# Last unit of a hybrid conv encoder step: W_in read as f32 and split on chip, another order of the gate pairs, later statistics of the first output tiles

## The chip, the cores and the metric

One core of one Trainium2 chip (trn2). The metric is the device time of one execution in microseconds (us). Three runs of the kernel before gave 1589.52, 1590.16 and 1591.43 us; their median is 1590.16 us. Engines: PE = TensorE (PEld its weight loads), DVE = VectorE, ACT = ScalarE, POOL = GpSimd, SP = SyncE, which here issues every DMA.

## What is computed

```python
hn = rms_norm(x, norm_g)                               # (4096 prompt + 32 sample rows, 1024)
proj = einsum('btd,de->bte', hn, w_in)                 # 1024 -> 3584, all f32
h_a, b_a, c_a, z_a, a_b, g_b, z_b = split(proj, 7)     # 512 wide each
conv_a = causal_dwconv(hist_a, c_a * h_a, conv_a_w)    # 3 taps
out_a = b_a * conv_a * silu(z_a)
v_b = a_b * sigmoid(g_b)
conv_b = causal_dwconv(hist_b, v_b, conv_b_w)          # 31 taps
s_b = silu(layer_norm(conv_b + bias, ln_b_g, ln_b_b))
out_b = s_b * silu(z_b)
y = x + concat([out_a, out_b]) @ w_out                 # then a final rms_norm
```

All inputs and outputs are f32. The new convolution histories are outputs too.

## The kernel before, in words

**Products.** Every f32 operand is split in a high part (a copy to fp32r, on ACT) and a low part (operand minus high part, on DVE or POOL); one product is three matmuls, high x high, high x low, low x high (`split_product`, L1733, its matmuls L1737 to L1739).

**Input projection.** 4140 columns of x (padding, sample, prompt) are 9 blocks of 460 columns. The 28 tiles of 128 output columns of `w_in` go in 14 pairs, in the order ORDER (L36): `ga` = g and a of group B, `hc` = h and c, `bz` = b and z, `zz` = two tiles of z_b, each with a number j from 0 to 3 (`zz`: 0 and 1). Unit 0 (periods 0 to 13) multiplies blocks 0 and 1 and also makes the forms of the weights: their split parts and the split sums of a seven-product scheme, eight chunks of 512 columns by two parts for each pair, which SP stores to DRAM as `weight_forms` (`store_forms`, L640) as two DMAs. Units 1 to 3 take two blocks each, with seven products for each pair (`strassen_product`, L1782). Unit 4, the last (periods III = 56 to 69, here called periods 0 to 13 of the last unit), takes block 8 alone: two tiles for each pair, each of two halves of 12 matmuls (`late_tile`, L1818), so 56 halves, numbered r. Each half reads one slot of the nine-slot ring `w_ring`; a slot holds 512 columns as high and low part, loaded from `weight_forms` (512 KB) by `load_late` (L663). Slots are reused nine halves later up to half 27, then only four slots turn (`late_slot`, L328), as the rest of that memory is taken for the output stage.

**What else goes on in the last unit.** ACT applies the function of the first tile of a pair (`evacuate`, L1160). DVE then multiplies the second tile in (`finish`, L1453): for `ga` one instruction (L1479), for `hc` one and three for the short convolution (L1503, L1506), for `bz` two (L1531, L1537). `zz` is ACT's alone. SP spills results to DRAM (`spill`, L670). The rest of DVE's time goes to the 31-tap convolution, one instruction per tap (L1554, the first L1551), each channel tile of a unit being a job of 31; `tap_quota` (L144) allows 12 per period, the first four before `finish`, and a job can begin one period after its `ga` pair. In ORDER the last unit's jobs 16 to 19 begin in its periods 1, 4, 8 and 11 and end in 3, 6, 10 and 13. POOL copies the history in front of each tile (`edges`, L945) and a `finish` waits for it. The first tap job of a pair waits for the same copy.

**Output stage.** Nine tiles of 512 rows (the last one is the sample). For each, layer norm over channels is 18 chained DVE steps and some on POOL, ACT and PE: `sums` and `sum_low` on POOL (L1006, L1017), `mean` on PE (L1847), `centre` on DVE (L1567), `squares` on ACT, `square_sums` and `var_low` on DVE (L1573, L1579), `var` on PE (L1851), `normalise` on DVE (L1585, L1590 to L1598), `silus` on ACT (L1224, L1228), `gate` (L1600), `mixed_b_high` on ACT (L1231), `b_low` (L1607). `a_low` (L1023, L1027) on POOL makes group A's low parts. For the first output tile all of this is placed in the last unit by hand: POOL's `sums` and `sum_low` in its period 3, PE's `mean` at the start of period 5 and `var` at the start of period 8, DVE's steps in the periods of `first_ln` (L1613). `W_out` is loaded, split and kept on chip (`out_weight_high`, `out_weight_low`) in periods 1 to 8.

Then nine steps (`run_steps`, L532) multiply row tiles of 128 rows (`rows_out`, L1878, 48 matmuls of 512 columns each), four to a step. PE's step L is: `mean(L+1)`, row tile 0, `var(L+1)`, row tiles 1, 2, 3. A row tile waits until DVE has added the residual of the tile two before (`need(pe, h_done, R - 1)`), and all row tiles of a step wait for its `b_low`. DVE's step L (L1693) is: `centre`, the finish of the last row tile, `square_sums`, `var_low`, `add_residual` of row tile 0, `normalise`, finish of 0, `add_residual` of 1, `gate`, finish of 1, `add_residual` of 2, `b_low`, finish of 2, `add_residual` of 3, where the layer norm is that of output tile L+1.

## Time and profile before

| | |
|---|---|
| median of three runs | 1590.16 us |
| the profiled execution: its time | 1589.94 us |
| its span in the trace | 1588.1 us |
| mean granted TensorE clock | 0.995 |
| PE busy | 1544.5 us, 97% |
| DVE busy | 1281.0 us, 81% |
| ACT, POOL busy | 509.0 us, 501.1 us, 32% each |
| DMA | 380 MB, mean 239 GB/s |

Times inside the trace count from the span's start. The profiled execution took 1.8 us more than its span. In the trace the last unit begins at about 1055.4 us and PE's last matmul of it starts at 1208.68 us; the output stage goes on to the end of the span. A line that shows "[idle <-releaser]" says how long the engine stood still before that instruction and what released it.

### The profile page before, as it was taken

Reading aid. Unit: us, or ns where it says so; the run is one execution under the profiler, and the core shown is the slowest. Engines: PE = TensorE matmul, PEld = TensorE weight load, DVE = VectorE, ACT = ScalarE, POOL = GpSimd, SP = SyncE. Lnnn points to the kernel's source line nnn. Section 1 sums busy time; section 2 is a strip of 40 time slices with the busy share of each in tenths; the row PEclk is TensorE's granted clock in tenths of the full one; section 3 lists DMA queues with packets and bytes.
Section 4 is the critical chain, followed back from the end, with each engine's and each line's share of the span. In section 5 each row is a group of like instructions: output and inputs, shape, how many; then the busy total and the mean of one; then the engine's idle time right before and its main releaser. Section 6 shows DMA issues by size and latency. Waiting matters only on the chain.

```text
span 1588.1 us, 19038 instructions
## 1 busy us (share of the span) xinstructions
PE 1544.5 (97%) x7196; PEld 1356.8 (85%) x7196; DVE 1281.0 (81%) x1196; ACT 509.0 (32%) x721; POOL 501.1 (32%) x434
## 2 busy tenths in 40 slices
PE   4899999999999999999999999999999999999998
PEld 4789999988888888888888888888887888888886
DVE  5699899997877998879798878785997777777752
ACT  4443433333333243332253312232231232323221
POOL 3756869201232221132221131113220333332310
PEclk9999999999999999999999999999999999999999
DMA  4898889689987788897779877779576443545441
GB/s 157 321 332 311 324 305 353 241 296 304 283 285 241 232 254 295 277 290 252 234 222 310 259 231 243 220 256 318 192 241 198 138 145 142 184 160 182 142 142 63
DMA packets 105613, 380.06 MB, mean 239 GB/s; under 512 B 16228, under 2 KB 20196, under 8 KB 101944
## 3 DMA queue, kind: packets, MB, share of 16 engines
q1 hardware_dynamic: 105528, 378.93, 71.4%
q8 instruction: 54, 0.88, 0.2%
q14 instruction: 31, 0.25, 0.0%
HBM read 277.70 MB, written 101.18 MB: 239 GB/s over the span
## 4 chain that ended last, share of the span: by engine, by line
PE 90%; DVE 6%; issue 2%; DMA 1%; POOL 1%; ACT 0%; POOLq 0%; DVEq 0%; SPq 0%; ACTq 0%
PE ps L1737 30%; PE ps L1739 30%; PE ps L1738 30%; DVE ps L1554 3%; DVE xf L1396 1%; DVE xf L1388 1%; DVE x_raw L1382 1%; DMA conv_b<-conv_spill 1%; DMA w_ring<-weight_forms 0%; PE ps L1844 0%; DVE w_ring L1396 0%; PE ps L1845 0%; POOL ln_tmp_a_f L1012 0%; POOL w_out_split L1032 0%; DVE conv_b L1571 0%
## 5 line engine op out<-in xcount | busy, mean ns | idle before, releaser
L1554 DVE SCALAR_TENSOR_TENSOR ps<-v,conv_b_taps,ps 128x920 f32<-128x920 f32 (+2 forms) x580 | 630.9, 1088 | 18.0
L1737 PE MATMUL ps<-xf,w_ring 128*128 128x460 f32 x1624 | 605.2, 373 | 3.3 <-DMA w_ring<-weight_forms 2.1
L1739 PE MATMUL ps<-xf,w_ring 128*128 128x460 f32 x1624 | 604.1, 372 | 0.0
L1738 PE MATMUL ps<-xf,w_ring 128*128 128x460 f32 x1624 | 602.7, 371 | 0.0
L1737 PEld LDWEIGHTS ps<-xf,w_ring 128*128 128x128 f32 x1624 | 306.4, 189 | 39.0 <-issue 3.3
L1738 PEld LDWEIGHTS ps<-xf,w_ring 128*128 128x128 f32 x1624 | 306.4, 189 | 34.7
L1739 PEld LDWEIGHTS ps<-xf,w_ring 128*128 128x128 f32 x1624 | 305.9, 188 | 35.1
L1172 ACT ACTIVATE sets<-ps 128x460 f32<-128x460 f32 x168 | 92.8, 552 | 460.3 <-PE ps L1739 456.5
L1737 PE MATMUL ps<-w_out_split,mixed 128*128 128x512 f32 x528 | 206.5, 391 | 0.0
L1739 PE MATMUL ps<-w_out_split,mixed 128*128 128x512 f32 x528 | 206.4, 391 | 0.0
L1738 PE MATMUL ps<-w_out_split,mixed 128*128 128x512 f32 x528 | 206.3, 391 | 0.0
L1002 POOL TENSOR_TENSOR sets<-sets 128x460 f32<-128x460 f32 x42 | 55.0, 1310 | 425.1 <-ACT sets L1172 425.1
L1737 PEld LDWEIGHTS ps<-w_out_split,mixed 128*128 128x128 f32 x528 | 99.5, 189 | 21.8 <-issue 1.0
L1739 PEld LDWEIGHTS ps<-w_out_split,mixed 128*128 128x128 f32 x528 | 99.5, 188 | 20.9
L1738 PEld LDWEIGHTS ps<-w_out_split,mixed 128*128 128x128 f32 x528 | 99.4, 188 | 20.8
L1342 ACT ACTIVATE ps<-h_rows 128x1024 f32<-128x1024 f32 (+1 forms) x33 | 34.0, 1029 | 213.6 <-DVE h_rows L1685 213.6
L879 POOL TENSOR_TENSOR row_mean_sq_eps<-row_mean_sq,rms_eps 128x1 f32<-128x1 f32 (+1 forms) x33 | 9.0, 274 | 282.2 <-ACT ps L1342 282.2
L1737 PE MATMUL ps<-xf 128*128 128x460 f32 x224 | 84.7, 378 | 10.8 <-DVE xf L1388 10.8
L1739 PE MATMUL ps<-xf 128*128 128x460 f32 x224 | 84.3, 376 | 0.0
L1738 PE MATMUL ps<-xf 128*128 128x460 f32 x224 | 83.6, 373 | 0.0
L905 POOL TENSOR_TENSOR x_raw<-x_raw,rstd_spread 128x460 f32<-128x460 f32 x56 | 69.4, 1272 | 44.9 <-DMA rstd_spread<-rstd_spill 44.9
L1685 DVE TENSOR_TENSOR h_rows<-ps,x_rows_again 128x1024 f32<-128x1024 f32 (+1 forms) x33 | 40.2, 1218 | 39.3 <-PE ps L1739 39.3
(144 smaller groups left out, 1575.0 us busy)
## 6 DMA issues: line engine op xcount, KB each, us to landing
w_ring<-weight_forms SPq DMA_DIRECT2D x350, 512.0 KB, 5.1
weight_forms<-xf SPq DMA_DIRECT2D x14, 2048.0 KB, 11.2
weight_forms<-w_ring SPq DMA_DIRECT2D x14, 2048.0 KB, 13.5
x_raw<-in_xT SPq DMA_DIRECT2D x18, 920.0 KB, 11.4
x_rows_again<-in_x_prompt SPq DMA_DIRECT2D x32, 512.0 KB, 4.3
out_y_prompt<-h_rows SPq DMA_DIRECT2D x32, 512.0 KB, 3.0
xf_f<-in_w_in SPq DMA_DIRECT2D x26, 512.0 KB, 6.3
x_row<-in_x_prompt SPq DMA_DIRECT2D x28, 460.0 KB
```

The lines of the kernel that those rows point to most:

```text
L905: pool.tensor_tensor(part, part, spread[:, 0:TB], ALU.mult).then_inc(x_scaled, 1)
L1002: pool.tensor_tensor(sets[:, s, QC, :], sets[:, s, QC, :], sets[:, s, QD, :], ALU.add).then_inc(c22_made, 1)
L1172: act.activation(sets[:, n % 2, quarter, :], ps[:, bank, 0:TB], ACT.Copy).then_inc(copied, 1)
L1342: act.activation(out_pair(2)[0:rows, :], hrow[0:rows, s, :], ACT.Square, scale=RMS_SCALE, accum_out=ssq[0:rows, s:s + 1]).then_inc(h_sumsq, 1)
L1382: dve.scalar_tensor_tensor(part, part, gain[:, k:k + 1], ps[:, FIRST_BANK[b], 0:TB], ALU.mult, ALU.mult).then_inc(x01_scaled, 1)
L1388: dve.tensor_tensor(standing_x(b, 1, 2 * r, 2 * r + 2), st[:, 2 * b + r // 2, 2 * (r % 2):2 * (r % 2) + 2, :], standing_x(b, 0, 2 * r, 2 * ...
L1396: dve.tensor_tensor(chunks(g, 2 * f, 2 * f + 2)[:, :, 1, :], raw_weights(g, f), chunks(g, 2 * f, 2 * f + 2)[:, :, 0, :].bitcast(F32), ALU. ...
L1554: dve.scalar_tensor_tensor(dst, window, wb[:, j, k:k + 1], part, ALU.mult, ALU.add).then_inc(taps_done, 1)
L1685: dve.tensor_tensor(hrow[0:rows, s, :], out_pair(s)[0:rows, :], raw[0:rows, s, :], ALU.add).then_inc(h_done, 1)
L1737: pe.matmul(out, ahi, bhi, start=(start and x == 0), stop=False, skip_group_check=goes_on)
L1738: pe.matmul(out, ahi, blo, start=False, stop=False, skip_group_check=goes_on)
L1739: mm = pe.matmul(out, alo, bhi, start=False, stop=(stop and x == len(terms) - 1), skip_group_check=goes_on)
```

## The change

In the last unit:

- SP loads 256 KB of `w_in` itself (f32) for each half, into the slot's low part; ACT copies it to the high part (`late_high`), POOL subtracts in place (`late_low`), and PE waits for POOL. 56 copies and 56 subtractions are new. `late_split` places them: while period g runs, the four halves of period g+1 (two before ACT's first `evacuate`, one after it, one at the end).
- The ring keeps nine slots up to half 44 and six after it.
- The pairs come in the order ORDER4: ga, hc, bz for each j, and the two `zz` pairs last. The tap plan follows: jobs 16 to 19 begin in periods 1, 4, 7, 10 and end in 3, 6, 9, 12, with 12, 12 and 7 taps in a cycle of three periods, 4 of them before `finish` where a job is under way.
- The first output tile's statistics move: `sums` to POOL's period 4, `mean` to period 7, `var` to period 11, DVE's `centre`, `square_sums`, `var_low` to 7, 8, 9, `normalise` to 12, `gate` to 13, `b_low` behind the unit. DVE takes these ahead of `finish`, not behind. `a_low(0)` and `sums(1)` are in POOL's period 13; `sum_high(1)` is ACT's last piece of the unit.
- In step 0 PE's `mean(1)` comes before row tile 1 and `var(1)` behind it.
- SP takes the ring load ahead of `store_convs` and `spill`.
- Unit 0 no longer stores chunk 2 of the forms, and stores chunks 0, 1 and 3 with two DMAs.

```diff
+ORDER4 = [(k, j) for j in range(4) for k in ("ga", "hc", "bz")] + [("zz", 0), ("zz", 1)]
...
-            return slot_of(PRODUCTS + r) if r < 28 else 5 + r % 4
+            return slot_of(PRODUCTS + r) if r < 45 else (1, 2, 5, 6, 7, 8)[(r - 45) % 6]
...
+        def late_split(n, part):
+            g = n - III
+            if g < 0:
+                return range(4) if part == 2 else ()
+            if g == G14 - 1:
+                return ()
+            return (range(4 * g + 4, 4 * g + 6), [4 * g + 6], [4 * g + 7])[part]
...
-                sp.dma_start(dst[:, 0:4], chunks(g, 0, 4).bitcast(F32)).then_inc(forms_out[0][g % 2], 16)
+                for a, b in ((0, 2), (3, 4)):
+                    sp.dma_start(dst[:, a:b], chunks(g, a, b).bitcast(F32)).then_inc(forms_out[0][g % 2], 16)
...
             def load_late(r):
                 if r < 9:
                     sp.wait_ge(product_done, PRODUCTS + r - 8)
                 else:
-                    sp.wait_ge(half_done, r - 8 if r < 28 else (r - 5 if r < 32 else r - 3))
-                load_ring(r // 4, r % 4, late_slot(r))
+                    sp.wait_ge(half_done, late_before(r) + 1)
+                g, f, c = ORDER.index(pair_of(III + r // 4)), r % 4 // 2, r % 2
+                src = A["w_in"][weight_tiles(g)[f]].rearrange("p (c m) -> p c m", c=2)[:, c]
+                sp.dma_start(ring_f32[:, late_slot(r), 1, :], src).then_inc(ring_in[late_slot(r)], 16)
...
                 for c in range(4):
+                    if late_after(4 * g + c) is not None:
+                        load_late(late_after(4 * g + c))
                     if c == 1:
                         store_convs(n)
                     if c == 2:
                         spill(n - 1)
-                    if late_after(4 * g + c) is not None:
-                        load_late(late_after(4 * g + c))
...
+            def late_low(r):
+                pool.wait_ge(late_hi, r + 1)
+                slot = late_slot(r)
+                pool.tensor_tensor(ring[:, slot, 1, :], ring_f32[:, slot, 1, :], ring[:, slot, 0, :].bitcast(F32),
+                                   ALU.subtract).then_inc(late_lo, 1)
...
+            for r in late_split(III - 1, 2):
+                late_low(r)
+
             for n in range(III, PERIODS):
...
-                if g == 3:
+                if g == 5:
+                    sum_low(0)
+                if g == 13:
+                    a_low(0, 0)
+                for part in range(3):
+                    for r in late_split(n, part):
+                        late_low(r)
+                    if part == 1 and 1 <= g <= KC:
+                        out_weight_low(g - 1)
+                if g == 4:
                     sums(0, 0)
-                    sum_low(0)
-                if g == 11:
+                if g == 13:
                     sums(1, 1)
                     sum_low(1)
...
+            def late_high(r):
+                slot = late_slot(r)
+                act.wait_ge(ring_in[slot], late_weights_in(r))
+                act.activation(ring[:, slot, 0, :], ring_f32[:, slot, 1, :], ACT.Copy).then_inc(late_hi, 1)
...
+                for r in late_split(n, 0):
+                    late_high(r)
...
+                if g == 5:
+                    sum_high(0)
+                if g == 12:
+                    mixed_a_high(0, 0)
+                if g == 13:
+                    silus(0, 0)
+                evacuate(n, 0)
+                for r in late_split(n, 1):
+                    late_high(r)
...
+                if g == 13:
                     mixed_b_high(0, 0)
                 evacuate(n, 1)
+                for r in late_split(n, 2):
+                    late_high(r)
+                if g == 7:
+                    squares(0, 0)
+                if g == 8:
+                    var_high(0)
+                if g == 13:
+                    sum_high(1)
...
-            first_ln = {5: centre, 6: square_sums, 7: var_low, 8: normalise, 10: gate, 12: b_low}
+            first_ln = {7: centre, 8: square_sums, 9: var_low, 12: normalise, 13: gate}
...
                 taps(TAPS_BEFORE[n])
-                finish(n - 1)
                 if n - III in first_ln:
                     first_ln[n - III](0, 0)
+                finish(n - 1)
                 taps(TAPS_AFTER[n])
...
             finish(PERIODS - 1)
+            b_low(0, 0)
...
-                    pe.wait_ge(ring_in[late_slot(r)], late_weights_in(r))
+                    pe.wait_ge(late_lo, r + 1)
...
-                if n == III + 5:
+                if n == III + 7:
                     pe.wait_ge(mean_w_ready, 1)
                     pe.wait_ge(taps_done, KB * 4 * JT)
                     mean(0)
-                if n == III + 8:
+                if n == III + 11:
                     var(0)
...
-                if n1:
-                    mean(L + 1)
+                late = 1 if isinstance(L, int) and L == 0 else 0
                 for r, (R, rs, _) in enumerate(row_tiles(L)):
+                    if n1 and r == late:
+                        mean(L + 1)
                     rows_out(L, s, r, R, rs)
-                    if n1 and r == 0:
+                    if n1 and r == late:
                         var(L + 1)
```

## Rows read from the trace of the kernel before

**Rows 1.** The page, busy time, share of the span and instructions of PE.

```profile
PE 1544.5 (97%) x7196; PEld 1356.8 (85%) x7196; DVE 1281.0 (81%) x1196; ACT 509.0 (32%) x721; POOL 501.1 (32%) x434
```

**Rows 2.** PE's waits from 1050 us on: total, times, longest.

```profile
PE ps L1844 <- DVE ln_tmp_b L1582: 3.6, 1, 3.6
PE ps L1844 <- issue: 3.1, 1, 3.1
PE ps L1737 <- DMA w_ring<-weight_forms: 2.1, 1, 2.1
PE ps L1844 <- POOL ln_tmp_a L1020: 1.9, 1, 1.9
```

**Rows 3.** Windows: PE, PEld, DVE, ACT, POOL busy (instructions), granted clock, DMA.

```profile
1055.40:1209.00 153.60, 146.07 (x676) 129.58 (x674) 128.46 (x175) 38.30 (x45) 35.11 (x22) 0.97 0.75 242
1105.00:1112.00 7.00, 5.14 (x18) 4.15 (x17) 2.10 (x3) 4.36 (x5) 6.26 (x6) 0.76 0.79 293
1140.00:1150.00 10.00, 6.67 (x20) 5.74 (x21) 8.96 (x13) 3.95 (x4) 5.44 (x4) 0.66 0.93 358
```

**Rows 4.** DVE's timeline in the last unit: start, us, line, instruction.

```profile
1109.83 0.76 DVE L1551 TENSOR_SCALAR ps<-v,conv_b_taps,conv_b_bias_sb 128x460 f32<-128x460 f32 x1 [13.24 <-POOL v L958]
1110.62 11.02 DVE L1554 SCALAR_TENSOR_TENSOR ps<-v,conv_b_taps,ps 128x460 f32<-128x460 f32 x15
...
1122.22 0.64 DVE L1537 TENSOR_TENSOR sets<-conv_a_acc,sets 128x460 f32<-128x460 f32 x1
1122.78 2.28 DVE L1571 TENSOR_TENSOR conv_b<-conv_b,ps 128x2048 f32<-128x2048 f32 x1
...
1133.68 0.63 DVE L1479 TENSOR_TENSOR u<-ps,sets 128x460 f32<-128x460 f32 x1
...
1136.19 1.22 DVE L1576 TENSOR_TENSOR ln_tmp_b_f<-ln_tmp_b_f,ln_tmp_a_f 128x1024 f32<-128x1024 f32 x1
...
1144.59 0.69 DVE L1590 TENSOR_SCALAR ln_tmp_a_f<-ps 128x512 f32<-128x512 f32 x1 [0.77 <-PE ps L1845]
...
1154.69 0.75 DVE L1551 TENSOR_SCALAR ps<-v,conv_b_taps,conv_b_bias_sb 128x460 f32<-128x460 f32 x1
```

**Rows 5.** ACT's timeline in the last unit.

```profile
1105.22 0.63 ACT L1216 ACTIVATE ln_tmp_a<-ln_tmp_a_f 128x512 fp32r<-128x512 f32 x1 [14.19 <-POOL ln_tmp_a_f L1015]
...
1162.06 2.92 ACT L1228 ACTIVATE conv_b<-conv_b,ln_b,ln_g 128x512 f32<-128x512 f32 x4
```

**Rows 6.** POOL's timeline, one 128x512 subtraction.

```profile
1105.93 1.27 POOL L1020 TENSOR_TENSOR ln_tmp_a<-ln_tmp_a_f,ln_tmp_a 128x512 fp32r<-128x512 f32 x1 [0.74 <-ACT ln_tmp_a L1216]
```

**Rows 7.** DMA issues from 1055 to 1209 us: count, KB each, us to landing.

```profile
conv_b<-conv_spill SPq DMA_DIRECT2D x8, 256.0 KB, 5.5
...
outa_spill<-sets SPq DMA_DIRECT2D x3, 230.0 KB, 3.2
```

**Rows 8.** Timelines of POOL (two) and DVE (one) where both engines run at once.

```profile
1229.67 4.63 POOL L1027 TENSOR_TENSOR mixed<-mixed_f,mixed 128x2048 fp32r<-128x2048 f32 x1 [0.59 <-ACT mixed L1202]
...
1247.68 3.22 POOL L1015 TENSOR_TENSOR ln_tmp_a_f<-ln_tmp_a_f 128x512 f32<-128x512 f32 x1
...
1229.87 4.98 DVE L1594 SCALAR_TENSOR_TENSOR ln_tmp_a_f<-ln_tmp_a_f 128x512 f32<-128x512 f32 x1
```

**Rows 9.** The chain that ended last, around step 0: start, us, what.

```profile
1212.81 0.23 PE ps L1737
...
1225.58 0.24 PE ps L1845
...
1258.76 0.24 PE ps L1845
1258.99 0.23 PE ps L1737
```

**Rows 10.** DVE's timeline in step 0: a residual added, and `b_low`.

```profile
1241.93 1.22 DVE L1685 TENSOR_TENSOR h_rows<-ps,x_rows_again 128x1024 f32<-128x1024 f32 x1
...
1256.14 2.29 DVE L1610 TENSOR_TENSOR mixed<-conv_b,mixed 128x2048 fp32r<-128x2048 f32 x1 [3.03 <-ACT mixed L1234]
```

More of the change, by code:

```diff
@@ L131, in period_of @@
 def period_of(k, u, j):
-    return u * G14 + ORDER.index((k, j))
+    return u * G14 + (ORDER4 if u == 4 else ORDER).index((k, j))
 JOBS = UNITS * JT
@@ L328, in late_slot, with late_before @@
         def late_slot(r):
-            return slot_of(PRODUCTS + r) if r < 28 else 5 + r % 4
+            return slot_of(PRODUCTS + r) if r < 45 else (1, 2, 5, 6, 7, 8)[(r - 45) % 6]
+        def late_before(r):
+            return max(p for p in range(r) if late_slot(p) == late_slot(r))
         def late_weights_in(r):
@@ L336, in late_after @@
         def late_after(p):
-            if p < 19:
-                return p + 9
-            if 22 <= p < 26:
-                return p + 6
-            return p + 4 if 28 <= p < 4 * G14 - 4 else None
+            return next((r for r in range(p + 1, 4 * G14) if late_slot(r) == late_slot(p)), None)
+        def late_split(n, part):
[5 more added lines that the diff above has]
+            return (range(4 * g + 4, 4 * g + 6), [4 * g + 6], [4 * g + 7])[part]
         const_in = sem("const_in")
@@ L739, in first_loads @@
                     load_first(mix1_f32[:, 0, JT:, :], zb_d, 0, j, first_zt)
-                if g == 8 and half == 0:
-                    sp.wait_ge(half_done, 22)
-                if g in (8, 9):
+                if g == 10 and half == 0:
+                    sp.wait_ge(half_done, 40)
+                if g in (10, 11):
                     load_first(cb1, conv_d, 1, j, first_cb[1])
@@ L1316, in _ @@
                     form_high(w, P6)
+            for r in late_split(III - 1, 2):
+                late_high(r)
             for n in range(III, PERIODS):
                 g = n - III
+                for r in late_split(n, 0):
+                    late_high(r)
                 if n == III:
                     gate_in_place(n - 1)
+                if g == 5:
[7 more added lines that the diff above has]
+                    late_high(r)
                 if 1 <= g <= KC:
                     out_weight_high(g - 1)
-                if g == 9:
-                    mixed_a_high(0, 0)
-                evacuate(n, 0)
-                if g in (3, 11):
-                    sum_high(g // 11)
-                if g == 5:
-                    squares(0, 0)
-                if g == 6:
-                    var_high(0)
-                if g == 9:
-                    silus(0, 0)
-                if g == 11:
+                if g == 13:
                     mixed_b_high(0, 0)
                 evacuate(n, 1)
+                for r in late_split(n, 2):
+                    late_high(r)
+                if g == 7:
[4 more added lines that the diff above has]
+                    sum_high(1)
             def row_square_out(R, s, rows):
```

27 lines of the change are left out of this document (14 added, 13 removed).

## The prediction, made before the changed kernel was run

> **What bounds the kernel now.** The page first: PE is busy 97% of the span [rows 1], so time can be had only where PE stands still or runs at a low clock. The waits of PE from 1050 us on say where that is [rows 2]: before the statistics of the first output tile (1.9 us for the mean, 3.6 us for the variance), once for a weight load (2.1 us), and 3.1 us at the end of the last unit. The windows give the rest [rows 3]: the last unit takes 153.6 us for 676 matmuls. At some 0.21 us each, the 20 matmuls of 1140 to 1150 us need 4.2 us and the wait is 3.6, so about 2.2 us went to a granted clock of 0.66; in the same way 1.3 us went at 1105 to 1112 us (0.76, that is part of it at 1.2 instead of 2.4 GHz). PE's own work in the unit is then 153.6 - 7.6 - 3.5 = 142.5 us, 10.1 us a period. The same window shows DVE busy 128.5 us, nearly as much. So DVE's timeline is read next [rows 4]: it lost 13.24 us in one piece, waiting for a history copy of POOL's that stood behind `sums`. It is the second bound of this unit, and the output stage cannot begin before its last piece, `b_low(0)`. The chain around step 0 shows what follows [rows 9]: the rows of step 0 begin at 1212.8 and those of step 1 at 1259.0 us.
>
> I count T from 1055.4 us. Before, step 0 begins at T = 157.4 and step 1 at T = 203.6.
>
> **PE's part.** The loads of 256 KB take about 5.5 us [rows 7] and are asked for nine or six halves ahead, 23 or 15 us at 2.5 us a half. A copy of 128x512 on ACT takes 0.63 us [rows 5], a subtraction on POOL 1.27 us [rows 6], both under 2.5. All together ACT gets 56 x 0.63 = 35 us on its 38, POOL 56 x 1.27 = 71 us on its 35 [rows 3], 106 of 142 us. Halves 0 to 3 are split behind ACT's last copies of unit 3, 5 us before they are wanted. The mean and the variance are now wanted 20 to 30 us later than DVE and POOL can have them. So the waits of 1.9, 3.6 and 2.1 us and the 3.5 us of slow clock go, and PE ends the unit at T = 142.5 instead of 153.6: 11 us to gain, if the next work is ready. SP takes ring loads ahead of its waits for DVE; behind those waits stand loads for 12 us later or more, so I cost the queue at nothing. Unit 0 gets 14 more issues on SP and 7 MB less of stores; PE waits for neither there, nothing either. If that cover failed, each late half would cost at most the missing load's 5.5 us.
>
> **DVE's timetable.** Taps are 11.02 / 15 = 0.73 us, so 12 take 8.9, 8 take 5.9, 4 take 2.9 and 3 take 2.2. `finish` takes 0.7 for ga, 2.5 for hc (1133.68 to 1136.19), 1.2 for bz; `centre` 2.2, the square sums 1.9 (1.2 and a half-wide one), `var_low` 0.7 (an instruction of the same form), `normalise` 10.1 (1144.59 to 1154.69) [rows 4]. A cycle ga, hc, bz has 31 taps and 27 us against PE's 30, so up to period 7 DVE waits for PE. It starts `centre` when PE's mean is there, T = 71.2. From there it has no more idle time: period 7 ends at 83.0 (2.2 + 0.7 + 8.9), 8 at 96.2 (2.9 + 1.9 + 2.5 + 5.9), 9 at 103.2 (2.9 + 0.7 + 1.2 + 2.2), 10 at 112.8, 11 at 124.1, the four taps of 12 at 127.0, `normalise` at 137.1, bz and 3 taps at 140.5. The four silus (2.9 us [rows 5]) are done by about then. `gate` 2.3, ACT's copy about 2, `b_low` 2.3 [rows 10]: T = 147.1. Even so PE would wait some 5 us at the end of the unit.
>
 Five DVE instructions, each behind one of these, part of the first hidden: 5.6 us. (b) hc in period 11 behind one: 1.4 us. (c) `a_low(0)` comes behind the last subtraction, T = 132 to 134, in `normalise`: 4.1 us, as in step 0 of before. (d) POOL's `sums(1)` waits for `normalise` and starts at once, bz's second instruction and so `gate` go behind it; ACT's `evacuate` of the last pair waits for that tile's spill (3.2 us [rows 7]) and `mixed_b_high` stands behind: 1.7 us. Sum 12.8 us. The row that is nearest for each is a full turn (the 4.98), so I take it; the bounds are 0 and, with two turns lost in places, 19. `b_low(0)` ends at T = 159.9, step 0 begins at 160.0, 2.6 us later than before. The 3.1 us wait at the end grows to some 17.
>
> **Step 0.** Before, `var(1)` is done at 1225.82 and `b_low(1)` at 1256.14 + 2.29 = 1258.43 [rows 9, 10]: 32.6 us, and step 1 starts 0.56 us later. This chain (`normalise`, finish of 0, residual of 1, silus, `gate`, finish of 1, residual of 2, `b_low`) sets the pace as much as PE does; there is no slack to take up a later variance. After the change `var(1)` stands behind row tile 1. A row tile takes (1258.5 - 1225.8) / 3 = 10.9 us, the first 12.5 with its slow clock. So `var(1)` is done at 160.0 + 12.5 + 0.5 + 10.9 + 0.5 = 184.4, `b_low(1)` at 217.0: step 1 starts at T = 217.0 instead of 203.6, 13.4 us late. Inside, row tile 3 waits for the residual of tile 1, which stands behind `normalise`: before it was added 17.3 us after `var(1)` (1243.16) and PE wanted it 22 us after; now PE wants it 10.9 us after, so PE stands 6 us there, and 2 more before step 1. That is in the 13.4. A wait of such length costs slow clock at its end, up to 1.6 us as at 1212.8 (12.5 against 10.9) if it is step 1's own first tile; the 2.1 us wait of before had none after it that I see. I take 1.0. From step 1 on the code is as before.
>
> **Sum.** 2.6 (step 0 later) + 10.8 (longer step 0) + 1.0 = 14.4 us on the profiled execution's 1589.94 us, which lies 0.2 us under the median: 1604.3 us. The point: PE's 11 us of waits go, and come back as a wait for `b_low(0)`, then a longer step 0.
>
> **Rivals.**
> 1. *The collisions fall on POOL.* If DVE mostly comes first, POOL waits, and has 36 us of room. Step 0 begins at T = 147.2, step 1 at 204.2: +0.6, with clock +1.6 at most, 1590.5 to 1592; half of the collisions makes 1597. For: POOL's addition of 3.22 us beside DVE's `gate` was POOL's turn to wait [rows 8]. Against: POOL comes in bursts and `a_low` is 4.6 us long. The Trainium skill ("SBUF — State Buffer", Who interferes with whom) says that issue order decides who blocks, and that the other blocks fully; by that rule both this and my forecast are open, and the sum would be 1590.5 where DVE always issues first. The trace agrees on the full block, 4.98 us.
> 2. *Faster.* As in 1, and `a_low(1)` also misses `normalise` in step 0, so that the chain from `var(1)` is 28.3 instead of 32.6 us: step 1 at T = 199.9, 3.7 us early, 1586.2 us. It decides on whether POOL's long `a_low` starts before or inside the chain; with `var(1)` a tile later, `a_low(1)` could be over before. Against: it waits for ACT, which waits for the residual of tile 0, 4 us before `normalise`, and lasts 4.6 us.
> 3. *PE starves.* POOL's 106 us grow by its own turns; if ACT is held in `var_high` or by a spill, halves come late. Over 15 us of lead must go first. Ten late halves at 1.27 us: 13 us more than the DVE chain only where both do not overlap; 1612 us.
> 4. *The waits do not go:* the mean or variance is still late. Then nothing is won at PE, but b_low(0) is the end anyway: 1604 again; it changes no number.
>
> **Numbers.** Forecast 0.56; rival 1 0.22 (0.17 of it within 0.2%); rival 2 0.14; rival 3 0.08. 0.2% (3.2 us) is about what a measurement of this kernel can tell from no change. Faster 0.14, same 0.17, slower 0.69. The range goes from 1589 to 1609 us: the lower end takes in rival 1, the upper one five more us of collisions; what is left out are rivals 2 and 3. The forecast's own range is 1597 to 1609 us.
>
> **What would show it.** PE's waits in the last unit at L1737 and L1844 gone; one wait of 10 us or more before the first row tile, released by DVE's `b_low`; a DVE step of `normalise` over 4 us in the last unit; hc's three in period 8 at twice their length; PE waits for `h_rows` before row tile 3 and for `b_low(1)` before step 1. Step 0 of 57 us instead of 46.2. The forecast is wrong if step 0 begins before T = 150, if POOL's durations rise instead of DVE's, or if PE waits for `w_ring` from POOL.

## The result, and the profile after

| | before | after |
|---|---|---|
| median, first series | 1590.8 us (1589.52 to 1592.7, 4 runs) | 1606.5 us (1604.2 to 1608.83, 4 runs) |
| ratio, first series | | 1.0094 [1.0075, 1.0114] |
| median, second series (last experiment) | 1591.01 us (17 runs) | 1603.98 us (6 runs) |
| ratio, second series | | 1.0084 [1.0064, 1.0105] |
| profiled execution: time, span | 1589.94, 1588.1 us | 1604.2, 1602.4 us |
| mean granted TensorE clock | 0.995 | 0.99 |

The change makes the kernel 13 to 16 us slower. The prediction said 1604.3 us, and that the waits of PE would come back in another place. The experiments below ran on three chips, each beside runs of before: their medians are 1590.21 us for 1 to 4, 1591.68 us for 5 to 7 and 1591.01 us for 8 and 9. Every ratio is to the runs of its own chip, so ratios compare better across experiments than medians do. Lines of `kernel.py` have moved: `rows_out`'s and the products' matmuls are L1790 to L1792 (before L1737 to L1739), mean and variance L1897 and L1898, `late_high` L1174, `late_low` L971, `centre` L1623, the square sums L1628 and L1629, the steps of `normalise` L1642 to L1650, `hc`'s three L1555 and L1558, `bz`'s second L1589, `b_low` L1662, `a_low` L1056.

The page of after, the busy times, the group of the new subtractions and the loads that feed them:

```profile
PE 1545.9 (96%) x7196; PEld 1357.8 (85%) x7196; DVE 1292.5 (81%) x1196; ACT 538.3 (34%) x777; POOL 578.2 (36%) x490
...
L971 POOL TENSOR_TENSOR w_ring<-w_ring_f,w_ring 128x512 fp32r<-128x512 f32 x56 | 75.5, 1365 | 48.0 <-ACT w_ring L1174 48.0
...
w_ring_f<-in_w_in SPq DMA_DIRECT2D x56, 256.0 KB, 3.1
```

Against [rows 1] PE's busy time is the same within 1.4 us, though the kernel takes 14 us more: PE stands. DVE is busy 11.5 us longer with the same 1196 instructions, so some of them got longer. POOL's subtractions have a mean of 1.365 us against 1.27 for the single one of [rows 6], so POOL also waited a little: 56 x 0.095 = 5 us in all.

PE's waits of after from 1040 us on (what it waited for: total, times, longest):

```profile
PE ps L1790 <- DVE mixed L1662: 16.2, 1, 16.2
PE ps L1790 <- DVE h_rows L1737: 5.8, 1, 5.8
PE ps L1790 <- issue: 1.7, 1, 1.7
```

None of the four waits of [rows 2] is left where it was. Instead there are one wait of 16.2 us for `b_low(0)`, one of 5.8 us inside step 0 and one of 1.7 us ahead of step 1. For the last the trace names no releaser ("issue"), but it ends at 1273.04, 0.1 us after `b_low(1)` (the last line of DVE below: 1270.65 + 2.29). The windows of after, the last unit and step 0:

```profile
1058.20:1200.00 141.80, 141.14 (x675) 126.41 (x673) 131.24 (x169) 58.37 (x87) 103.93 (x75) 1.00 0.57 166
1215.40:1273.00 57.60, 49.94 (x198) 40.18 (x198) 30.46 (x24) 13.17 (x16) 15.05 (x11) 0.89 0.32 112
```

PE runs the unit in one piece at a granted clock of 1.00: its last matmul starts at 1198.98, and then it waits. What it waits for is seen in DVE's timeline of after: the pieces of the first output tile's layer norm, and the instructions of DVE that took longer than their form takes alone.

```profile
1129.41 2.28 DVE L1623 TENSOR_TENSOR conv_b<-conv_b,ps 128x2048 f32<-128x2048 f32 x1
...
1145.32 1.68 DVE L1629 TENSOR_TENSOR ln_tmp_b_f<-ln_tmp_b_f 128x512 f32<-128x512 f32 x1
...
1147.58 1.95 DVE L1555 TENSOR_SCALAR conv_a_acc<-u,conv_a_taps 128x460 f32<-128x460 f32 x1
1149.56 3.26 DVE L1558 SCALAR_TENSOR_TENSOR conv_a_acc<-u,conv_a_taps,conv_a_acc 128x460 f32<-128x460 f32 x2
...
1178.54 0.61 DVE L1555 TENSOR_SCALAR conv_a_acc<-u,conv_a_taps 128x460 f32<-128x460 f32 x1
...
1192.86 4.98 DVE L1646 SCALAR_TENSOR_TENSOR ln_tmp_a_f<-ln_tmp_a_f 128x512 f32<-128x512 f32 x1
...
1204.37 2.41 DVE L1589 TENSOR_TENSOR sets<-conv_a_acc,sets 128x460 f32<-128x460 f32 x1
...
1213.11 2.29 DVE L1662 TENSOR_TENSOR mixed<-conv_b,mixed 128x2048 fp32r<-128x2048 f32 x1 [1.98 <-ACT mixed L1275]
...
1241.08 0.69 DVE L1642 TENSOR_SCALAR ln_tmp_a_f<-ps 128x512 f32<-128x512 f32 x1 [2.57 <-PE ps L1898]
1241.81 4.66 DVE L1643 TENSOR_SCALAR ln_tmp_a_f<-ln_tmp_a_f 128x512 int32<-128x512 int32 x1
...
1270.65 2.29 DVE L1662 TENSOR_TENSOR mixed<-conv_b,mixed 128x2048 fp32r<-128x2048 f32 x1 [3.02 <-ACT mixed L1275]
```

And POOL's timeline of after in period 8 and at `normalise`:

```profile
1146.41 2.86 POOL L1061 TENSOR_TENSOR w_out_split<-w_out_split_f,w_out_split 128x1024 fp32r<-128x1024 f32 x1
1149.23 4.75 POOL L971 TENSOR_TENSOR w_ring<-w_ring_f,w_ring 128x512 fp32r<-128x512 f32 x3
...
1192.23 5.05 POOL L1056 TENSOR_TENSOR mixed<-mixed_f,mixed 128x2048 fp32r<-128x2048 f32 x1
```

Read the two side by side. DVE's 4.98 us step begins 0.6 us after POOL's 5.05 us `a_low` and ends 0.6 us after it, at 1197.84: it does its own 0.69 us once POOL is through. In period 8, `W_out`'s subtraction ends at 1149.27 and `hc`'s first instruction, 1.95 us instead of 0.46, at 1149.53; the two behind it take 3.26 us instead of 1.43 beside the three subtractions of the weights.

**Where the 14.3 us of span went**, with T counted as in the prediction (the unit begins at 1057.95 us in after):

| | before | after | difference |
|---|---|---|---|
| beginning of the last unit | 1055.40 | 1057.95 | +2.5 |
| from there to step 0's first row tile (T) | 157.4 | 157.6 | +0.2 |
| step 0 | 46.2 | 57.5 | +11.3 |
| step 1 to the end of the span | 329.1 | 329.4 | +0.3 |

The beginning of step 0 and its `mean(1)`, behind row tile 0, in PE's timeline of after, and the beginning of step 1 in its chain of waits:

```profile
1215.54 0.76 PE L1790 MATMUL ps<-w_out_split,mixed 128*128 128x512 f32 x1 [16.20 <-DVE mixed L1662]
...
1228.99 0.40 PE L1897 MATMUL ps<-ln_tmp_a,mean_w 128*128 128x512 f32 x1
```

```profile
1271.32 1.72 issue
1273.04 0.47 PE ps L1790
```

The gain at PE (12.3 us: the unit's last matmul at T = 141.0 instead of 153.3) is fully taken up by the wait for `b_low(0)`, and the loss lies in step 0. The first row, 2.5 us ahead of the unit, was not foreseen; the last two experiments are about it.

### The profile page after: what moved, and what is told of

Its sections match the earlier page's. It is cut to its first block and busy times, and to the rows that moved or that the text cites. A ratio compares the mean times of both kernels' runs of the same rounds, so it can differ in the third digit from the quotient of the medians.

```text
span 1602.4 us, 19163 instructions
## 1 busy us (share of the span) xinstructions
PE 1545.9 (96%) x7196; PEld 1357.8 (85%) x7196; DVE 1292.5 (81%) x1196; ACT 538.3 (34%) x777; POOL 578.2 (36%) x490
## 5 line engine op out<-in xcount | busy, mean ns | idle before, releaser
L1790 PE MATMUL ps<-xf,w_ring 128*128 128x460 f32 x1624 | 603.7, 372 | 0.8 <-DVE v L1524 0.3
L1792 PE MATMUL ps<-xf,w_ring 128*128 128x460 f32 x1624 | 603.0, 371 | 0.0
L1790 PEld LDWEIGHTS ps<-xf,w_ring 128*128 128x128 f32 x1624 | 305.4, 188 | 36.1 <-issue 0.9
L1792 PEld LDWEIGHTS ps<-xf,w_ring 128*128 128x128 f32 x1624 | 304.9, 188 | 34.9
L1213 ACT ACTIVATE sets<-ps 128x460 f32<-128x460 f32 x168 | 92.8, 552 | 457.2 <-PE ps L1792 453.4
L1790 PE MATMUL ps<-w_out_split,mixed 128*128 128x512 f32 x528 | 208.0, 394 | 23.8 <-DVE mixed L1662 16.2
L1792 PE MATMUL ps<-w_out_split,mixed 128*128 128x512 f32 x528 | 207.4, 393 | 0.0
L1790 PEld LDWEIGHTS ps<-w_out_split,mixed 128*128 128x128 f32 x528 | 100.3, 190 | 46.9 <-issue 25.9
L1792 PEld LDWEIGHTS ps<-w_out_split,mixed 128*128 128x128 f32 x528 | 100.1, 190 | 21.2
L1790 PE MATMUL ps<-xf 128*128 128x460 f32 x224 | 85.9, 383 | 10.8 <-DVE xf L1440 10.8
L971 POOL TENSOR_TENSOR w_ring<-w_ring_f,w_ring 128x512 fp32r<-128x512 f32 x56 | 75.5, 1365 | 48.0 <-ACT w_ring L1174 48.0
L1792 PE MATMUL ps<-xf 128*128 128x460 f32 x224 | 85.2, 380 | 0.0
L1791 PE MATMUL ps<-xf 128*128 128x460 f32 x224 | 84.8, 378 | 0.0
```

What stands on the lines that cost most here:

```text
L971: pool.tensor_tensor(ring[:, slot, 1, :], ring_f32[:, slot, 1, :], ring[:, slot, 0, :].bitcast(F32), ALU.subtract).then_inc(late_lo, 1)
L1213: act.activation(sets[:, n % 2, quarter, :], ps[:, bank, 0:TB], ACT.Copy).then_inc(copied, 1)
L1790: pe.matmul(out, ahi, bhi, start=(start and x == 0), stop=False, skip_group_check=goes_on)
L1791: pe.matmul(out, ahi, blo, start=False, stop=False, skip_group_check=goes_on)
L1792: mm = pe.matmul(out, alo, bhi, start=False, stop=(stop and x == len(terms) - 1), skip_group_check=goes_on)
```

## The experiments

For the sum inside the unit one measure is the same in all of them and has no part of PE or of the loads in it: the time from DVE's `centre` to the start of `b_low(0)`. In after it is 1213.11 - 1129.41 = 83.7 us.

**1. The changed kernel with step 0's old order.**

```diff
-                late = 1 if isinstance(L, int) and L == 0 else 0
+                late = 0
```

> The changed kernel with one part undone: in step 0 PE issues the mean of the next output tile before row tile 0 and its variance behind it, as before. Main theory (the chain from the variance to b_low(1) sets the length of step 0, so a variance one row tile later costs 11 us): step 0 goes from 57.5 back to about 46.5 us, the waits of PE for h_rows (5.8 us) and before step 1 (1.7 us) go, the start of step 0 moves about 1.5 us later since sum_low(1) ends 1.1 us after b_low(0); in all 9 to 10 us less than the changed kernel, about 1594 to 1596 us. Rival (the length of step 0 comes from DVE being late and the clock after 16 us of idle PE, not from the place of the variance): step 0 stays over 54 us, total within 3 us of the changed kernel.

Measured: 1596.87 us (1594.68 to 1598.83, 6 runs), ratio to before 1.0045 [1.0029, 1.006], against 1.0094 and 1.0084 for after. PE's waits from 1040 us on are a single one; behind it, in its timeline, stands the mean:

```profile
PE ps L1897 <- POOL ln_tmp_a L1049: 17.4, 1, 17.4
```

```profile
1218.66 0.76 PE L1897 MATMUL ps<-ln_tmp_a,mean_w 128*128 128x512 f32 x1 [17.39 <-POOL ln_tmp_a L1049]
```

From the start of `b_low(0)` to that of `b_low(1)` it is 1263.93 - 1215.11 = 48.8 us against 1270.65 - 1213.11 = 57.5 in after: 8.7 us less, and the wait for `h_rows` is gone. The medians differ by 9.6 us with the first series of after and by 7.1 with the second, by the ratios it is 6 to 8 us. So most of the loss is this one order. It isn't all of the 11.3: `sum_low(1)` on POOL is last now, so the mean starts 1.3 us behind the end of `b_low(0)`, which is at 1217.40, and the first row tile begins at the low clock after the wait: twelve of its matmuls take some 0.6 us, where before had eight of them from 1213.6 us on. Rival 2 of the prediction, that `a_low(1)` misses `normalise`, fell in both orders: a step of 4.99 us here, of 4.66 us in after.

**2. The kernel before with step 0's new order**, and nothing else of the change.

```diff
-                if n1:
-                    mean(L + 1)
+                late = 1 if isinstance(L, int) and L == 0 else 0
                 for r, (R, rs, _) in enumerate(row_tiles(L)):
+                    if n1 and r == late:
+                        mean(L + 1)
                     rows_out(L, s, r, R, rs)
-                    if n1 and r == 0:
+                    if n1 and r == late:
```

> The kernel before with only this part of the change: mean(1) and var(1) of step 0 one row tile later. Main theory: step 0 grows from 46.2 to 57 us, PE waits about 6 us for h_rows before row tile 3, total about 1600 to 1602 us (10 to 11 more than before, half a us less because mean(1) is no longer ahead of the rows). Rival (with DVE free at the start of step 0 the later variance is absorbed): under 3 us more, 1593 at most.

Measured: 1602.56 us (1598.56 to 1604.6, 4 runs), ratio 1.0072 [1.0047, 1.0097], 12.4 us over before by the medians. Of the five lines of PE's waits of this kernel, the first two (the other three are much as in [rows 2]; of the 5.1 us, 3.5 are the old wait at the unit's end and 1.6 stand ahead of step 1):

```profile
PE ps L1737 <- DVE h_rows L1685: 5.8, 1, 5.8
PE ps L1737 <- issue: 5.1, 2, 3.5
```

Step 0 goes from 1216.77 to 1273.42: 56.7 us instead of 46.2, with the same 5.8 us wait for the residual of row tile 1. The step's length is therefore the order's doing, with the old weights, the old tap plan and the old place of `b_low(0)` as well.

**3. `a_low(0)` earlier.** ACT's copy for it behind its first `evacuate` of period 11, `a_low(0)` at the end of POOL's period 11.

```diff
-                if g == 12:
-                    mixed_a_high(0, 0)
...
                 evacuate(n, 0)
+                if g == 11:
+                    mixed_a_high(0, 0)
...
-                if g == 13:
+                if g == 11:
                     a_low(0, 0)
```

> The changed kernel with ACT's copy and POOL's a_low of the first output tile moved from periods 12 and 13 to period 11 of the last unit, while DVE does taps. Main theory (a_low's 4.6 us stand in DVE's normalise, and normalise is on the chain to b_low(0)): the 4.98 us step of normalise shrinks to under 2, b_low(0) ends 3.5 to 4.3 us earlier, total about 1600 us. Rival (PE's 16 us wait hides it, or the copy collides elsewhere with the three of hc): b_low(0) moves by less than 1.5 us, total over 1602.5.

Measured: 1607.59 us (1606.15 to 1610.28, 4 runs), ratio 1.0118 [1.0095, 1.014]. Nothing is won: the rival came true, with `hc`'s three as the new victims. The timelines of DVE and of POOL of this kernel:

```profile
1180.98 6.59 DVE L1558 SCALAR_TENSOR_TENSOR conv_a_acc<-u,conv_a_taps,conv_a_acc 128x460 f32<-128x460 f32 x2
```

```profile
1180.64 4.78 POOL L1056 TENSOR_TENSOR mixed<-mixed_f,mixed 128x2048 fp32r<-128x2048 f32 x1
```

`normalise` is free of it, and `hc`'s two taps take 6.59 us instead of 1.43: 5.2 us, taken from other DVE instructions with both inputs in SBUF. From `centre` to `b_low(0)` it is now 1215.52 - 1130.31 = 85.2 us, 1.5 more. Moving a long POOL instruction helps only if it lands beside work that it doesn't hold up, such as the taps of the 31-tap convolution, which read PSUM (experiment 4).

**4. The split on the chip undone**, with the new order of pairs, tap plan, ring and statistics kept. SP loads the ready forms of 512 KB from DRAM as before, ACT and POOL have none of the 56 pieces, unit 0 stores all four chunks.

```diff
-                for a, b in ((0, 2), (3, 4)):
+                for a, b in ((0, 2), (2, 4)):
...
-                src = A["w_in"][weight_tiles(g)[f]].rearrange("p (c m) -> p c m", c=2)[:, c]
-                sp.dma_start(ring_f32[:, late_slot(r), 1, :], src).then_inc(ring_in[late_slot(r)], 16)
+                load_ring(ORDER.index(pair_of(III + r // 4)), r % 4, late_slot(r))
...
             def late_low(r):
+                return
...
             def late_high(r):
+                return
...
-                    pe.wait_ge(late_lo, r + 1)
+                    pe.wait_ge(ring_in[late_slot(r)], late_weights_in(r))
```

> The changed kernel with the split on chip undone: the last unit loads split forms (512 KB) again through the same nine then six slots, the 56 copies on ACT and 56 subtractions on POOL are gone, order of the pairs, statistics and step 0 stay as changed. Main theory (the subtractions collide with DVE's instructions of two SBUF inputs): the square sums and hc's three in period 8 take 4.4 instead of 8.7 us, b_low(0) ends about 4.5 to 5 us earlier, the wait of PE before step 0 falls from 16 to about 11.5 us, total about 1599.5 us. a_low's and sums' collisions stay. Rival (the split is hidden, the late b_low is the order's doing alone): b_low(0) where it was, total within 1.5 us of the changed kernel; or a DMA wait shows and takes it back.

Measured: 1594.95 us (9 runs), ratio 1.0043 [1.0024, 1.0062]. Eight of the nine lie between 1593.74 and 1604.38 us; one took 3119.3 us, which nothing on record explains, and the ratio leaves it out. PE's waits of this kernel from 1040 us on:

```profile
PE ps L1790 <- DVE mixed L1662: 8.2, 1, 8.2
PE ps L1790 <- DVE h_rows L1737: 5.8, 1, 5.8
PE ps L1790 <- issue: 2.0, 1, 2.0
```

From `centre` to `b_low(0)` it is 1203.43 - 1126.99 = 76.4 us: 7.3 less than after, where the prediction of this run had 4.5 to 5. Of these, 2.6 are period 8 (square sums and `hc` from 8.7 to 6.0 us), and 4.6 are `normalise`, in which no step takes over 0.7 us. That is the surprise, since `a_low(0)` is here, too. ACT's and then POOL's timeline of this kernel:

```profile
1173.10 1.91 ACT L1243 ACTIVATE mixed<-mixed_f 128x2048 fp32r<-128x2048 f32 x1
```

```profile
1175.09 4.80 POOL L1055 TENSOR_TENSOR mixed<-mixed_f,mixed 128x2048 fp32r<-128x2048 f32 x1 [24.53 <-ACT mixed L1243]
```

and ACT's timeline of after at the same place:

```profile
1185.13 0.63 ACT L1174 ACTIVATE w_ring<-w_ring_f 128x512 fp32r<-128x512 f32 x1 [5.19 <-DMA w_ring_f<-in_w_in]
1185.66 1.90 ACT L1243 ACTIVATE mixed<-mixed_f 128x2048 fp32r<-128x2048 f32 x1
```

Here `a_low(0)` lies beside twelve taps, and they take 8.81 us as everywhere. With the split two things stand ahead of it. ACT's copy of group A comes at 1185.7 instead of 1173.1, since a weight copy ahead of it waits 5.19 us for its load. But that copy ends at 1187.6, and `a_low(0)` starts only at 1192.23, without idle time, behind POOL's last subtraction, which is ahead of it in POOL's queue. What released that one shows in ACT's and then in POOL's timeline of after:

```profile
1189.35 0.56 ACT L1207 ACTIVATE sets<-ps 128x460 f32<-128x460 f32 x1 [0.82 <-PE ps L1792]
1189.80 0.62 ACT L1174 ACTIVATE w_ring<-w_ring_f 128x512 fp32r<-128x512 f32 x1
```

```profile
1190.50 1.77 POOL L971 TENSOR_TENSOR w_ring<-w_ring_f,w_ring 128x512 fp32r<-128x512 f32 x1 [0.61 <-ACT w_ring L1174]
```

The subtraction waits for ACT's copy of the last half, that copy stands behind ACT's second `evacuate` of period 12, and that one waited for PE. So the wait that ends last at `a_low(0)` is the order in POOL's queue, and no load. The late copy of group A alone, over at 1187.6, would also have let `a_low(0)` reach into `normalise`; no run takes away the one and leaves the other, nor puts `a_low(0)` ahead of period 12's subtractions. The weights themselves were early enough: PE never waited for one.

**5. Experiment 4 with step 0's old order** (`late = 0`).

> Two parts of the change undone together: split forms loaded again in the last unit (as in the run with forms loaded, which put b_low(0) 8 us earlier), and the mean and variance of step 0 back to the places of before. What stays is the order of the pairs, the ring of nine then six slots and the later statistics. If the two effects add (8 us at b_low(0), 11.3 us in step 0 less 1.6 us of waiting for sum_low(1)): about 1585 to 1587 us, faster than the kernel before by 0.2 to 0.3%, step 0 46 to 47 us long. Rival (they share a cause, so the second gives little once the first is there): 1591 us or more.

Measured: 1584.38 us (1583.06 to 1590.7, 12 runs), ratio 0.9953 [0.9935, 0.9972]: faster than before by 7.3 us (1591.68 us on this chip). Its one wait of PE from 1040 us on:

```profile
PE ps L1897 <- POOL ln_tmp_a L1048: 9.3, 1, 9.3
```

`b_low(0)` starts at 76.45 us after `centre` as in 4, and step 0 (from one `b_low` to the next) takes 1253.99 - 1205.89 = 48.1 us, near the 48.8 of 1. From `centre` to the end of the span the profiled executions take 473.0 us in after, 464.6 in 1, 465.2 in 4 and 456.5 here: 8.4 and 7.8 us less one by one, 16.5 us less together. So the two causes add, and what is left of the change, above all the new order of the pairs with the late statistics, is a gain.

**6. Experiment 5, and two pieces moved behind `b_low(0)`.** The last three taps before the end go behind `b_low(0)`, and ACT makes `sum_high(1)` ahead of `mixed_b_high`.

```diff
                 finish(n - 1)
-                taps(TAPS_AFTER[n])
+                if n != PERIODS - 2:
+                    taps(TAPS_AFTER[n])
...
             b_low(0, 0)
+            taps(TAPS_AFTER[PERIODS - 2])
             taps(TAPS_LEFT)
...
                 if g == 13:
+                    sum_high(1)
                     mixed_b_high(0, 0)
...
-                if g == 13:
-                    sum_high(1)
```

> As the run before it, and the last three taps of the last convolution job moved behind b_low(0), where DVE stands idle for the mean, with ACT's sum_high(1) ahead of mixed_b_high so that the mean of step 0 waits for nothing behind b_low(0). If DVE's chain alone sets the start of step 0: b_low(0) 1.7 to 2.2 us earlier, in all 2 to 3.5 us less, about 1583 us. If another wait ends there (the silus on ACT, or the spill that evacuate of the last pair waits for): under 1 us less.

Measured: 1583.0 us (1580.8 to 1591.94, 12 runs), ratio 0.9944 [0.9927, 0.9962]. The median is 1.4 us under that of 5; their intervals overlap, so only the traces say that it is a gain. The profiled execution is the slowest of the twelve (1591.94 us) and reaches `centre` 7.4 us later than that of 5, so only what comes behind `centre` is compared; from there to the end of the span it is 453.4 us, 3.1 less. There `b_low(0)` starts 75.4 us after `centre` (1.1 less, where three taps are 2.2: `gate` now stands behind POOL's `sums` and takes 3.28 us), `centre(1)` comes 4.35 instead of 4.78 us after `b_low(0)` has started, and from one `b_low` to the next it is 1258.13 - 1212.21 = 45.9 us instead of 48.1. PE's waits of this kernel from 1040 us on:

```profile
PE ps L1898 <- ACT sets L1207: 5.2, 1, 5.2
PE ps L1791 <- DVE mixed L1661: 0.7, 1, 0.7
```

The 9.3 us wait of 5 is now 0.7 us for `b_low(0)` and 5.2 us for ACT. The latter is for the last `evacuate` of the unit, which PE awaits ahead of the output stage and which stands behind `mixed_b_high`: it ends at 1212.6 us, when POOL's `sum_low(1)` has been done for 1.1 us. This kernel has the lowest median of all that ran.

**7. POOL's turns without its work.** The low part of a late weight is a second copy by ACT; POOL subtracts 2 of its 512 columns. The low parts of the last unit's weights are so left out of the result.

```diff
-                act.activation(ring[:, slot, 0, :], ring_f32[:, slot, 1, :], ACT.Copy).then_inc(late_hi, 1)
+                act.activation(ring[:, slot, 0, :], ring_f32[:, slot, 1, :], ACT.Copy)
+                act.activation(ring[:, slot, 1, :], ring_f32[:, slot, 1, :], ACT.Copy).then_inc(late_hi, 1)
...
-                pool.tensor_tensor(ring[:, slot, 1, :], ring_f32[:, slot, 1, :], ring[:, slot, 0, :].bitcast(F32),
-                                   ALU.subtract).then_inc(late_lo, 1)
+                pool.tensor_tensor(ring[:, slot, 1, 0:2], ring[:, slot, 1, 0:2].bitcast(F32),
+                                   ring[:, slot, 0, 0:2].bitcast(F32), ALU.subtract).then_inc(late_lo, 1)
```

> The changed kernel with POOL's 56 subtractions cut from 512 to 2 columns; ACT copies the weights to the low part too (56 copies more), so the low parts of the last unit's weights are left out of the result, and loads, copies on ACT, waits and order stay. Separates POOL's time at DVE's SBUF operands from the rest of the split. If those collisions are the split's whole price, as in the forecast: the square sums and hc's three of period 8 take about 5 instead of 8.7 us and b_low(0) is 8 us earlier as in the run with forms loaded. If the place of a_low counts too (ACT's copies wait for their loads and hold back ACT's copy for a_low until normalise runs): only about 4 us earlier, with one step of normalise still at 4 to 5 us, total about 1602 us. If the split costs nothing there: no change.

Measured: 1600.03 us (1597.4 to 1604.6, 9 runs), ratio 1.0047 [1.0025, 1.0069]. DVE's and then POOL's timeline of this kernel (its L1647 is L1646 of after, and the line ahead of `a_low(0)` is the last subtraction, of 2 columns):

```profile
1190.76 5.00 DVE L1647 SCALAR_TENSOR_TENSOR ln_tmp_a_f<-ln_tmp_a_f 128x512 f32<-128x512 f32 x1
```

```profile
1189.99 0.20 POOL L971 TENSOR_TENSOR w_ring<-w_ring 128x2 fp32r<-128x2 f32 x1 [2.48 <-ACT w_ring L1175]
1190.14 5.07 POOL L1056 TENSOR_TENSOR mixed<-mixed_f,mixed 128x2048 fp32r<-128x2048 f32 x1
```

From `centre` to `b_low(0)` it is 1208.85 - 1127.61 = 81.2 us, 2.5 less than after. Period 8 takes 6.6 instead of 8.7 us, and what is left there is `W_out`'s subtraction; but `normalise` still loses its step to `a_low(0)`, since POOL's last subtraction, short as it is, still waits for ACT's last weight copy, behind PE. So of the 7.3 us that the split costs inside the unit, about 2.5 are the time of POOL's subtractions and about 4.8 the place of `a_low(0)` behind them. The expectation had the step at 5 us right. The reason that it gave, that late loads hold back ACT's copy of group A, isn't what ends last: that copy is done at 1185.8 us, 4.4 us before `a_low(0)` starts.

**8 and 9. After and before once more, unaltered, with more rounds.** In the first profiles 2.5 us of the difference had arisen before the last unit, near 60 us, where the change does little.

> The changed kernel once more, unaltered, in more rounds, beside the kernel before. Open is whether the 2.5 us that its profiled execution lost between 55 and 62 us (a granted clock of 0.77 in the window 50 to 65 us against 1.00 before) belong to the change. Main theory: they do not; either kernel shows this dip in some of its executions and not in others. Then the change itself costs 11.8 us (0.3 for the start of step 0, 11.3 for its length, 0.3 behind it), and with many executions of both the difference of the medians comes out at 11 to 13.5 us, a ratio of 1.007 to 1.0085. Rival: the change makes the dip the rule (for instance by its other stores in unit 0). Then the difference of the medians is 14 to 16 us, a ratio of 1.009 to 1.010. From 50 to 65 us the profile shows 1.00 or 0.77 by chance under the first and 0.77 under the second; PE's waits of 16 and 5.8 us in the output stage are unchanged under both.

> The kernel before, unaltered, as a kernel of its own: what two series of the same kernel on one chip differ by, and a second profile of it. Main theory (the dip between 55 and 62 us comes to any kernel by chance): ratio 0.999 to 1.001, and where its profile shows 0.77 in the window 50 to 65 us, the last unit begins about 2.5 us later than in the first profile, with step 0 again 46.2 us long. Rival (the dip belongs to the change): this profile shows 1.00 there.

Measured: after 1603.98 us (1600.85 to 1609.68, 6 runs), ratio 1.0084 [1.0064, 1.0105]; before 1592.17 us (1588.91 to 1595.4, 12 runs), ratio to the shared runs of before 1.0006 [0.9993, 1.0018]. The window of 50 to 65 us of after's first profile, and of its second:

```profile
50.00:65.00 15.00, 10.93 (x38) 9.10 (x39) 8.50 (x5) 5.19 (x7) 6.88 (x4) 0.77 0.91 357
```

```profile
50.00:65.00 15.00, 11.21 (x51) 9.46 (x52) 8.23 (x5) 5.25 (x8) 7.16 (x5) 1.00 0.94 363
```

and of the second profile of before, whose first showed 1.00 in this window:

```profile
50.00:65.00 15.00, 10.49 (x35) 8.68 (x36) 8.93 (x5) 5.62 (x7) 7.16 (x5) 0.77 1.04 429
```

Each kernel shows both clocks, as the main theory had it. The second profile of after has a span of 1599.1 us with the unit at 1055.2, the second of before one of 1590.2 us with the unit at 1058.2. So 2.5 to 3 us at the start are no part of the change: like is compared with like by 1599.1 against 1588.1 (11.0 us) and 1602.4 against 1590.2 (12.2 us). In after's second profile step 0 begins at T = 157.6 again and takes 57.0 us, and `b_low(0)` starts 83.65 us after `centre`, against 83.70. In before's second one it is 45.3 us from `mean(1)`, at 1215.80, to step 1, at 1261.05, where the first has 46.9 by the same measure (from 1212.10 to 1258.99). So the expected "again 46.2 us" missed by 1.6 us: the wait ahead of `mean(1)` was 1.9 instead of 3.1 us here, and no slow matmuls followed it.

## Why the prediction was right, and where its terms were off

**What held.** All of PE's old waits went and PE ended its unit at T = 141.0 (predicted 142.5). `centre` came at T = 71.5 (71.2). The wait before step 0 was 16.2 us ("some 17"), released by `b_low`, as predicted. PE stood 5.8 us before row tile 3 ("6 us") and 1.7 before step 1 ("2 more"). A step of `normalise` took 4.98 us. Step 0 took 57.5 us ("57"). Its chain came out piece by piece: from the start of step 0 to DVE's first step behind `var(1)`, at 1241.08, 25.5 us (24.4 predicted), from there to the end of `b_low(1)` 31.9 (32.6). Experiments 1 and 2 show the cause from both sides: undone in after it gives back 8.7 us, done alone in before it costs 10.5 in step 0.

**The term of the collisions was mis-sized**: 12.8 us forecast, 10.8 measured. By places: (a) period 8, 4.3 instead of 5.6; (b) `hc` in period 11, 0.15 instead of 1.4; (c) `a_low(0)`, 4.55 instead of 4.1; (d) `bz`'s second instruction, 1.8 instead of 1.7. I had taken a full turn for each instruction. That holds where a long POOL instruction runs (c, d). Where both engines have a row of short ones, DVE lost less than that, and in period 11 POOL was nearly through when `hc` came. So step 0 began 0.2 us later than before, not 2.6 as in "2.6 (step 0 later)".

**The clock term**, 1.0 us, measured 0.3: the first matmul behind the 1.72 us wait took 0.47 us, the second 0.23 again, so no stretch of low clock followed there. The 16.2 and 5.8 us waits did have one behind them (the granted clock of step 0 is 0.89). The one behind 5.8 us falls in row tile 3, and DVE's chain hides it: PE still stood 1.7 us for `b_low(1)`. The one behind 16.2 us isn't hidden, as `var(1)` now stands behind the slow row tile: that tile took 13.4 us up to `mean(1)` (1215.54 to 1228.99) instead of the 12.5 taken from before.

**Step 0's own term** was 0.5 us short: 11.3 against 10.8. The way to `var(1)` took 1.1 us more, 0.9 of it by that slow stretch; the way from there took 0.7 less, as DVE had added the residual of row tile 0 earlier and stood free; and PE went on 0.1 us behind `b_low(1)`, where the sum had nothing (and the text 0.56).

By these measured terms the change costs 0.2 + 11.3 + 0.3 = 11.8 us, 2.6 less than the sum of 14.4. The profiled time of 1604.2 us still lies at the forecast, since that execution had the 2.5 us at the start, which no term foresaw and which isn't the change's. That the two agree to 0.1 us is luck. The error of the sum is these 2.6 us, and the second series (13.0 us between the medians) lies between the two.

**The place of `a_low(0)`.** The prediction put it into `normalise` because POOL's last subtraction is ahead of it, at T = 132 to 134. That came out: it started at T = 134.3 without idle time behind that subtraction (experiments 4 and 7). SP's queue was costed at nothing, and for PE that held, too. ACT did wait for late loads (5.19 us at one copy), which the sum had nowhere; at `a_low(0)` that was not the wait that ended last.

**The rivals.** Rival 1 (POOL waits, DVE doesn't) fell: DVE lost 10.8 us in the unit, POOL's 56 subtractions 5 us in all. The Trainium skill ("SBUF — State Buffer", Who interferes with whom) leaves it to the issue order who is blocked; the trace agrees, with both directions in it: at the 4.98 us step POOL had begun 0.6 us before DVE, and in period 8 both engines had instructions that took longer than alone (DVE's 1.95 us, POOL's `W_out` subtraction 2.86 instead of 2.41). Rival 2 (faster) fell with the 4.66 us step in step 0. Rival 3 (PE starves) fell: there is no wait of PE for a weight in the last unit; loads took 3.1 us, not 5.5. Rival 4 (the waits stay) fell with the list of waits.

**Where the meant gain is.** It is there: with the forms loaded and step 0's old order, the same order of pairs and the same late statistics run 7.3 us faster than before (experiment 5; 8.7 us with 6, both against before's 1591.68 us). The split and the late `mean(1)` and `var(1)` took it away.

## What to carry to other kernels

- Before a piece is moved out of a busy engine's way, read the chain behind it. The variance of the first output tile cost PE a wait of 3.6 us where it stood in the unit; `var(1)` in step 0 cost none, and moving it by one row tile cost a row tile, since 32.6 us of DVE's chain hang on it in a step of 46.
- Work that is free by the busy times (POOL at 36%, ACT at 34%) is paid for by DVE's instructions with two inputs in SBUF, and by whatever stands behind it in its own engine's queue. A long POOL instruction wants to lie beside DVE work that reads PSUM (4.80 us of `a_low(0)` beside the taps cost DVE nothing in experiment 4); check where it lands after each change, and what now stands ahead of it in its own queue.
- When one engine's waits are taken out at the end of a stage, compute first when the second-busiest engine can be done: here at T = 147, with collisions 157, against PE's 141.

## What was unexpected of the hardware

- The loads of 256 KB landed after 3.1 us in the median, where the 256 KB loads of [rows 7] had taken 5.5. The same loads as there, `conv_b<-conv_spill`, landed after 4.1 us in the last unit of after, where the DMA engines were busy 0.57 of the time against 0.75. That the lighter traffic is the reason isn't shown.
